# Moving the sample's branch combination and copy between units on VectorE, and one load on the queue, in a hybrid decoder step

## The reference

```
o_c = einsum(p_c, v_cmp)          # compressed branch
o_s = einsum(p_s, v_sel blocks)   # selected branch
o_w = einsum(p_w, v_win)          # sliding window of 512
yb  = gates[...,0]*o_c + gates[...,1]*o_s + gates[...,2]*o_w
br_b = (silu(zb) * yb) @ w_out_b
```

## Time and profile before

| | |
|---|---|
| median of 3 runs | 2444.23 us (2441.23 to 2445.5) |
| the profiled execution, its own time | 2440.02 us |
| its span | 2438.2 us |
| PE busy | 2361.2 us, 97% |
| DVE busy | 1226.6 us, 50% |
| ACT busy | 987.0 us, 40% |
| POOL busy | 208.4 us, 9% |
| mean granted clock of TensorE | 0.994 |

### The profile page before, as it was taken

The page is one execution under the profiler, slowest core; times in us unless marked ns, Lnnn a source line. Parts: engine busy times, 40 slices in busy tenths (PEclk is TensorE's granted clock), DMA queues, the critical chain, the costliest instruction groups (busy, mean ns, idle before and its releaser), DMA issues.

```text
span 2438.2 us, 45791 instructions
## 1 busy us (share of the span) xinstructions
PE 2361.2 (97%) x18087; PEld 2067.9 (85%) x18087; DVE 1226.6 (50%) x2325; ACT 987.0 (40%) x2023; POOL 208.4 (9%) x349
## 2 busy tenths in 40 slices
PE   8999999999999999999989999999999999998998
PEld 8999999997788655589989999999977885555998
DVE  4444232546675566564454432224557656665543
ACT  4332223435564455533233221234446445554332
POOL 0000000000000233410000000000000002333000
PEclk9999999999999999999999999999999999999999
DMA  6343354707542667663234334547086318867530
GB/s 236 121 138 104 87 169 124 162 19 159 85 55 35 104 118 124 126 197 114 93 118 138 121 104 101 165 115 162 8 174 84 53 17 137 124 105 172 158 113 38
DMA packets 293310, 279.12 MB, mean 114 GB/s; under 512 B 92601, under 2 KB 281465, under 8 KB 291816
## 3 DMA queue, kind: packets, MB, share of 16 engines
q1 hardware_dynamic: 288680, 239.34, 44.2%
q0 software_dynamic: 4416, 36.85, 4.1%
HBM read 249.25 MB, written 43.53 MB: 120 GB/s over the span
## 4 chain that ended last, share of the span: by engine, by line
PE 87%; DVE 5%; ACT 3%; SPq 1%; issue 1%; DMA 1%; DVEq 1%; POOL 0%; ACTq 0%
PE ps L772 47%; PE ps L1016 13%; PE ps L942 7%; PE ps L1143 3%; PE ps L1167 2%; PE ps L1126 2%; PE ps L969 2%; DVE chL L2139 2%; PE ps L1265 2%; PE ps L1041 1%; ACT chH L1657 1%; PE ps L1413 1%; DMA w_raw<-in_w_out_b 1%; PE ps L1273 1%; SPq L570 1%
## 5 line engine op out<-in xcount | busy, mean ns | idle before, releaser
L772 PE MATMUL ps<-hH,wH 128*128 128x272 f32 x2016 | 418.5, 289 | 8.4 <-DVE hL L1982 8.4
L772 PE MATMUL ps<-hH,wL 128*128 128x272 f32 x2016 | 420.3, 290 | 0.0
L406 DVE TENSOR_TENSOR wL<-w_raw,wH 128x2048 fp32r<-128x2048 f32 (+1 forms) x107 | 246.3, 2302 | 341.7 <-ACT wH L397 339.3
L772 PE MATMUL ps<-hL,wH 128*128 128x272 f32 x2016 | 417.1, 288 | 0.0
L772 PEld LDWEIGHTS ps<-hH,wH 128*128 128x128 f32 x2016 | 318.3, 189 | 10.3 <-issue 7.5
L772 PEld LDWEIGHTS ps<-hH,wL 128*128 128x128 f32 x2016 | 317.0, 189 | 0.0
L772 PEld LDWEIGHTS ps<-hL,wH 128*128 128x128 f32 x2016 | 316.9, 189 | 0.0
L2139 DVE TENSOR_TENSOR chL<-ps,chH 64x256 fp32r<-64x256 f32 x512 | 216.5, 423 | 159.0 <-ACT chH L1657 151.4
L1657 ACT ACTIVATE chH<-ps 64x256 fp32r<-64x256 f32 x512 | 207.1, 404 | 214.3 <-PE ps L1016 205.8
L397 ACT ACTIVATE wH<-w_raw 128x2048 fp32r<-128x2048 f32 (+1 forms) x107 | 204.8, 1914 | 93.4 <-PE ps L772 77.6
L742 POOL TENSOR_SCALAR pr<-pr,inv,zg 128x512 f32<-128x512 f32 (+3 forms) x256 | 153.0, 607 | 963.4 <-DVE inv L2329 963.4
(11 more groups left out here) (344 smaller groups left out, 4041.7 us busy)
## 6 DMA issues: line engine op xcount, KB each, us to landing
w_raw<-in_w_in SPq DMA_DIRECT2D x59, 1024.0 KB
craw<-in_cache_kv SPq DMA_DIRECT2D x256, 128.0 KB, 5.2
w_raw<-in_w_in SPq DMA_DIRECT2D x64, 256.0 KB
k_sel<-in_cache_kv SPq DMA_DIRECT2D x128, 128.0 KB, 5.2
v_sel<-in_cache_kv SPq DMA_DIRECT2D x128, 128.0 KB, 9.6
out_new_win_sample<-in_state_win POOLq DMA_DIRECT2D x16, 1016.0 KB, 6.1
w_raw<-in_w_out_a SPq DMA_DIRECT2D x8, 1024.0 KB
k_win<-in_state_win SPq DMA_DIRECT2D x16, 512.0 KB, 6.4
```

The lines of the kernel that those rows point to most:

```text
L406: dve.tensor_tensor(block_part(wL, b), block_part(w_raw, b), block_part(wH, b).bitcast(F32), ALU.subtract).then_inc(w_lo, 1)
L772: last = nc.tensor.matmul(ps[:, bank + hf, 0:HALF], st, x[:, k, hf * HALF:(hf + 1) * HALF], start=k == 0 and w is wH and x is xH, stop=k = ...
```

## The change

SP: in the last pair's turn the value loads are issued first, and `zbs` after them; each keeps its own wait. DVE: the three weight instructions move from k = 3 to k = 2 (behind `maxima`), the first `sy` instruction joins the other two at k = 4, and in blocks with a back pair `inverses` and `turned` of unit k = 7 are done in unit k = 6 ahead of the copy into `yT`.

```diff
@@ SP
+                sp.wait_ge(s_fin, 4 * l + 3)
+                load_half(l, 3, numbers, 3, v_sel, v_win, s_v)
                 sp.wait_ge(sa_kt, 48 * l + 48)
                 sp.dma_start(zbs[:], a["zb_keep"][l].rearrange("k p t -> p k t")).then_inc(zb_back, 16)
-                sp.wait_ge(s_fin, 4 * l + 3)
-                load_half(l, 3, numbers, 3, v_sel, v_win, s_v)
@@ DVE
-                def combine_first(pair, bank):
+                def combine_gains(pair):
...
                     dve.tensor_tensor(small[:, 80:83], grow[:, pair, :], small[:, 76:79], ALU.mult)
+
+                def combine(pair, bank):
+
+                    dve.wait_ge(sa_yt, 4 * l + pair)
                     dve.drain()
-                    dve.wait_ge(sa_yt, 4 * l + pair)
                     dve.tensor_scalar(sy[:], ps[:, bank, 0:P], small[:, 80:81], None, ALU.mult)
-
-                def combine_rest(bank):
-
                     for n in (1, 2):
...
-                    if i:
+                    if i and (k < 7 or back is None):
                         inverses(i)
                         turned(i - 1)
...
-                    if k == 3 and back is not None:
-                        combine_first(back, 6 + (mm + 1) % 2)
+                    if k == 2 and back is not None:
+                        combine_gains(back)
                     if k == 4 and back is not None:
-                        combine_rest(6 + (mm + 1) % 2)
+                        combine(back, 6 + (mm + 1) % 2)
...
                     if k == 6 and back is not None:
+                        inverses(i + 1)
+                        turned(i)
                         copy_turned(mm)
```

## The result

Six runs of the changed kernel have a median of 2452.69 us (2451.76 to 2453.74), six of the kernel before 2444.01. The ratio is 1.0038 with a 95% interval of 1.0028 to 1.0049: +9.3 us, between +6.8 and +12.0. The forecast was +6.0. It was slower, at the places that the forecast named; but its terms for the queue and the clock were too small, it shared the loss out wrongly between the weights and `zbs`, and one mechanism was missing. The profiled executions are 2440.02 us before and 2452.02 after; executions of one kernel spread over up to 10 us, so I read the traces from marks inside a layer, and the main mark is v, the issue of the last pair's values.

The account below looks back on a forecast made before the run. The attention's end was taken to hang on the DMA queue. Terms -2.0 + 2.2 + 3.0 + 1.0 + 1.8 summed to +6.0 us, 2450.2 us on the median, range 2443 to 2457.

Parts of the forecast that it names:

- the queue: Loads at the attention's end: 1.10 us of transfer time left unused, so output weights land 1.1 us later per layer.
- the clock: PE after idling at `output(57)`: layer 0 would get layer 1's low clock, +1.0 us.
- The weights' term: First output weights at the attention's end land 1.1 us later in each layer, +2.2 us in all.
- the term for `zbs` and the lock: Before unit 58: `zbs` lands late, POOL's products and DVE's split hold each other up; +3.0 us.
- covers hold: Rival: `zbs` lands early enough or POOL and DVE pass each other; about +1.8 us, 2446.0; chance 0.26.
- blocks 2 and 4: DVE's moves in these attention blocks of both layers gain 0.5 us a block, -2.0 us in all.
- tail: Unit 62, attention's end: `bH` starts later, `output(63)` follows later; +0.9 us a layer, 1.8 in all.
- The step at k = 3: PE's 1.28 us idle before `output(k = 3)` shrinks, but ACT's exponentials hold the next step; about 0.1 us is left.
- Block 6's gain: It ends in the same layer's queue chain, which starts before it, so it counts as nothing.
- served in their order of issue: DMA queue at the attention's end: transfers of `zbs`, values and weights are served as they were issued.
- POOL becomes the bound: Rival: `zbs` lands together with the weights, POOL's products and one split end late; +13.3 us, 2457.5; chance 0.13.

Follow-up runs that it names:

- after_ob1_held: Changed kernel, but second output weights and `gb` issued only once ACT has split the first; ratio 1.0046 to the kernel before, +11.2 us.
- after_products_60: Changed kernel with POOL's seven products of `zbs` ahead of unit 60 instead of 58; ratio 1.0079 to the kernel before, +19.3 us.
- after_split_58: Changed kernel with the split of the first output weights moved one unit later, to unit 58; ratio 1.0045 to the kernel before, +11.0 us.
- dve_only: Changed kernel with the old load order, so only DVE's moves; ratio 0.9992 to the kernel before, -2.0 us.
- combine_only: Kernel before with branch weights at k = 2 and their product at k = 4, nothing else moved; ratio 0.9997 to it, -0.7 us.
- loads_only: Kernel before with only the load order changed, values ahead of `zbs`; ratio 1.0033 to it, +8.1 us.
- after_held_shared: Changed kernel with second output weights and `gb` held back and four of POOL's seven products on DVE; ratio 1.0026 to the kernel before, +6.4 us.

## Why the prediction was right, and where its sizes were off

The sign held, and so did the outline of the mechanism: the values' wait goes, the queue gives it back at the weights and at `zbs`. The total is less of a success than it looks. The weights' term was too small by a factor of four, the term for `zbs` and the lock was too large on the chain that ended last, and the stated range, 2443 to 2457, also holds the point of the rival "covers hold", 2446.0. By its terms, in us, with the traces of before and after:

| term | forecast | measured |
|---|---|---|
| blocks 2 and 4, two layers | -2.0 | -3.0 |
| unit 58 later than v (weights +2.2, late `zbs` +3.0) | +5.2 | +4.6 + 5.2 = +9.8 |
| clock | +1.0 | +1.7 + 0.6 = +2.3 |
| tail | +1.8 | +1.9 |
| sum | +6.0 | +11.0 |

The profiled pair differs by 12.0 us; the 1.0 us that the table lacks lies outside these places, where the edit changes nothing. The timed runs differ by 9.3 (6.8 to 12.0).

*How the +9.8 is made up.* In both traces DVE's `inv` releases POOL's unit 58. On that chain the weights' landing, behind v, gives 3.7 + 4.9 = 8.6 us, and the longer way from the landing to unit 58 (6.46 and 6.26 against 5.59 and 5.92) gives 1.2. The forecast had 2.2 and 3.0. POOL's own chain, `zbs` and the stretched products, ended 0.37 us earlier in both layers and would have cost nearly the same by itself; that is why neither after_ob1_held, which relieves the weights, nor after_products_60, which takes the lock away, brings unit 58 back to where it was.

*Blocks.* 0.75 us a block instead of 0.5. The step at k = 3 was right: 0.23 measured where I had 0.1, with ACT's exponentials next. The copies at k = 6 gave 0.5, the whole of the 0.53 us, and not all of their time came back before `maxima`. Block 6's gain ended at the gate of the queue, as forecast.

*Load order.* This is the step that failed: "the weights stand behind the same bytes as before" and so land 1.1 us later. They landed 3.7 and 4.9 later behind v: 8.6 us in the sum that had 2.2. Part of that is the execution of before: its landing in layer 1, v + 30.0, is the earliest of six of the old order, and the values' own landing varies from + 25.9 to + 30.9 in those, which no run here explains. Against their mean it is 2.4 and 4.0. Of it 1 to 1.7 us are, by difference, the slow start, near the forecast; another 1 to 2 us, shown by the two kernels that hold the next weights back, are what I hadn't seen: as PE has its values early, `s_fin` of the last pair rises while the first weights are still on their way, and 3 MB more enter the queue behind them. A wait taken away opened another gate too soon. It also answers the forecast's "served in their order of issue": loads issued behind the weights held these back, so the queue doesn't keep that order strictly. The start left far more than 1.1 us of engine time unused (share 0.43 over 6 us), and much of it was caught up.

*Late `zbs`.* Forecast for v + 28.8 and + 27.0, it came at + 30.3 and + 30.1. The lock was as forecast in kind, with 2.0 us on POOL and 0.7 and 0.5 on DVE where I had 2.29 and 0.6 and 0.2. But POOL was not the end of the chain, as the forecast had it: DVE's `inv` came 0.37 us later. The Trainium skill's rule in "SBUF — State Buffer", section "Who interferes with whom", is borne out by the four traces in which the seven products take 10.65 to 10.67 us beside the split and one of them 3.3; what each side pays shows only in the durations apart and together. The rival "POOL becomes the bound" was nearer than its 0.13: after_ob1_held and after_split_58 show that bound itself. It is a tie, and I had treated it as an either-or.

*Clock.* Right in place, too small. Unit 58 to `output(63)`, less the tail's 0.97, took 15.04 and 14.93 us against 13.36 at full clock. The longer idle time doesn't explain the size: of the six kernels in the old order with the split at its old place, PE idle for only 2.1 to 2.6 us at `output(57)` of layer 1, two kept a clock of 1.00 and lost nothing there (dve_only and combine_only), and four lost 1.0 to 1.5 us; loads_only, idle for 7.5 and 7.2, lost 1.3 and 1.6. What decides it stays open.

*Tail.* Right, in size too: idle of 1.60 us at `output(63)` against 0.48, `bH` later, +0.97 us a layer.

Open: why the rate of the value loads differs between executions, how much of the weights' lateness is the slow start, and whether the two edits add exactly; the intervals are too wide.

## What to carry to other kernels

When a wait is taken away, list every gate that the waiting engine opens afterwards: here PE's earlier end released 3 MB into the queue in which the next needed transfer stood. A large load with long rows at the head of a queue can be the cover that keeps the DMA engines busy while small ones are issued; moving it back can cost their start as well as its own lateness (here 1 to 1.7 us a layer, by difference). Work that looks like a stall on one engine (a split that waits for its weights) may be the hidden place for it: before moving it, read in which order the other engine does its part. And where two chains end within half a microsecond, shortening one is worth no more than the distance to the other.

## What the runs showed of the hardware

- A POOL product of two SBUF operands and a DVE instruction of two SBUF operands hardly overlap: seven products shared between both took 5.7 us where one after the other is 6.6 (after_held_shared). The cost lands on either side: one POOL product of 3.3 us instead of 1.27, DVE's split 2.4 to 3.1 instead of 2.29. In the changed kernel DVE's small instruction on `sums` (128x2) took 0.35 us beside a running product, and 0.16 without one in the kernel before.
- The first six microseconds of value loads alone moved 107 GB/s at a DMA share of 0.43 in layer 0 and 116 GB/s at 0.69 in layer 1, though SP issued them back to back; behind `zbs` the same six microseconds moved 332 GB/s at 0.97 and 321 at 0.94.
- In one queue, holding back 3 MB issued behind the first weights made these land 1 to 2 us earlier (after_ob1_held, after_held_shared).
- After 8.8 us of idle time PE ran at 0.50 (1.2 of 2.4 GHz) although fully busy, and unit 58 to `output(63)` became 1.6 us longer. After 2.1 to 2.6 us of idle time at the same place the clock fell in four of six executions, which cost 1.0 to 1.5 us, and stayed at 1.00 in two.
